# Two stacked transformer blocks on one core: the next stage's first weights are loaded and split at another place

## What is computed

```python
def first_block(...):                       # two layers
    for i in range(DEPTH):
        a = rms_norm(h, attn_norm[i])
        proj = a @ w_in[i]                  # differential attention, SSD and GLA mixers
        ...
        h = h + mix @ w_out[i]
        f = rms_norm(h, ffn_norm[i])
        h = h + (jax.nn.silu(f @ w_ffn_gate[i]) * (f @ w_ffn_up[i])) @ w_ffn_down[i]
        h = h + jax.nn.sigmoid(h @ ple_w_gate[i]) * (p[i] @ ple_w_proj[i])

def second_block(...):                      # four layers: sb, moba, swa, sb
    for i in range(DEPTH_2):
        mod = c_act @ ada_w[i] + ada_b[i]
        sh1, sc1, g1, sh2, sc2, g2 = ...    # split of mod
        h = modulate(rms_norm_2(x, norm_gain[i, 0]), sh1, sc1)
        y = one of stick_breaking / moba / swa_sink attention
        x = x + g1 * y
        h = modulate(rms_norm_2(x, norm_gain[i, 1]), sh2, sc2)
        x = x + g2 * swiglu(h, ffn_w_gate[i], ffn_w_up[i], ffn_w_down[i])
```

## Time and profile before

| | |
|---|---|
| median of three runs | 2336.67 us (2335.86 to 2341.69) |
| the profiled execution | 2342.8 us, span 2341.0 us |
| granted PE clock, mean | 0.979 |
| PE matmul busy | 2185.9 us, 93% |
| PE weight loads busy | 2075.4 us, 89% |
| DVE busy | 1598.4 us, 68% |
| ACT busy | 1092.3 us, 47% |
| chain that ended last | PE 80%, DVE 9%, ACT 5%, DMA 2%, DVE's and SP's queues 3% |
| memory read | 433.82 MB, 186 GB/s over the span |

### The profile page before, as it was taken

One profiled execution on the slowest core, in us unless ns is written; L12 is line 12 of the kernel. 1 busy time (PEld: TensorE's weight loads), 2 busy tenths in 40 slices (PEclk: granted clock), 3 DMA queues, 4 the chain that ended last, 5 costly groups with the idle time before them and its releaser, 6 DMA issues.

```text
span 2341.0 us, 44967 instructions
## 1 busy us (share of the span) xinstructions
PE 2185.9 (93%) x17588; PEld 2075.4 (89%) x17588; DVE 1598.4 (68%) x2655; ACT 1092.3 (47%) x1752; POOL 0.2 (0%) x4
## 2 busy tenths in 40 slices
PE   5889999998899999898999999999988999998998
PEld 4779899987798999898999888999887999897998
DVE  4676587756756877566778766778777854666554
ACT  3545444445454443455444455544465444555443
POOL 0000000000000000000000000000000000000000
PEclk8999999999999999999999999999999999999999
DMA  4464399934653998444599544699543965542664
GB/s 125 107 162 147 104 303 300 292 100 110 166 158 104 302 299 282 117 143 138 189 301 297 184 145 131 215 300 298 169 127 122 291 193 166 144 134 83 191 185 135
DMA packets 545379, 436.40 MB, mean 186 GB/s; under 512 B 27472, under 2 KB 470904, under 8 KB 545144
## 3 DMA queue, kind: packets, MB, share of 16 engines
q1 hardware_dynamic: 541904, 431.21, 60.5%
q10 hardware_dynamic: 3368, 3.71, 0.5%
HBM read 433.82 MB, written 1.05 MB: 186 GB/s over the span
## 4 chain that ended last, share of the span: by engine, by line
PE 80%; DVE 9%; ACT 5%; DMA 2%; DVEq 2%; issue 1%; SPq 1%; ACTq 1%
PE bank L644 12%; PE bank L646 12%; PE bank L645 12%; PE acc L644 7%; PE acc L646 7%; PE acc L645 7%; PE bank L788 3%; PE bank L1160 2%; PE bank L844 2%; ACT w_hi L1284 2%; DVE w_lo L1734 1%; PE bank L654 1%; PE bank L709 1%; PE bank L710 1%; PE bank L713 1%
## 5 line engine op out<-in xcount | busy, mean ns | idle before, releaser
L1284 ACT ACTIVATE w_hi<-wslot 128x1024 fp32r<-128x1024 f32 x590 | 610.5, 1054 | 534.2 <-PE acc L646 253.5
L644 PE MATMUL bank<-h_hi,w_hi 128*128 128x256 f32 x2784 | 792.5, 285 | 27.3 <-DVE w_lo L1734 10.6
L645 PE MATMUL bank<-h_lo,w_hi 128*128 128x256 f32 x2784 | 778.3, 280 | 0.0
L646 PE MATMUL bank<-h_hi,w_lo 128*128 128x256 f32 x2784 | 778.3, 280 | 0.0
L1734 DVE TENSOR_TENSOR w_lo<-wslot,w_hi 128x1024 fp32r<-128x1024 f32 x412 | 494.2, 1221 | 219.4 <-ACT w_hi L1284 218.8
L644 PEld LDWEIGHTS bank<-h_hi,w_hi 128*128 128x128 f32 x2784 | 525.7, 189 | 45.4 <-DVE w_lo L1728 14.1
L645 PEld LDWEIGHTS bank<-h_lo,w_hi 128*128 128x128 f32 x2784 | 529.1, 190 | 2.2 <-issue 1.7
L646 PEld LDWEIGHTS bank<-h_hi,w_lo 128*128 128x128 f32 x2784 | 526.5, 189 | 0.0
L644 PE MATMUL acc<-mid_hi,w_hi 128*128 128x256 f32 x1120 | 317.7, 284 | 7.8 <-DVE mid_lo L2279 4.6
L646 PE MATMUL acc<-mid_hi,w_lo 128*128 128x256 f32 x1120 | 312.6, 279 | 0.0
L645 PE MATMUL acc<-mid_lo,w_hi 128*128 128x256 f32 x1120 | 312.6, 279 | 0.0
(11 more groups left out here) (286 smaller groups left out, 2987.1 us busy)
## 6 DMA issues: line engine op xcount, KB each, us to landing
wslot<-in_ada_w_dram SPq DMA_DIRECT2D x192, 512.0 KB, 5.7
wslot<-in_ffn_w_gate_dram SPq DMA_DIRECT2D x88, 512.0 KB, 4.9
wslot<-in_ffn_w_up_dram SPq DMA_DIRECT2D x88, 512.0 KB, 5.4
wslot<-in_ffn_w_down_dram SPq DMA_DIRECT2D x88, 512.0 KB, 3.7
wslot<-in_w_in_dram SPq DMA_DIRECT2D x72, 512.0 KB, 4.8
wslot<-in_sb_w_in_dram SPq DMA_DIRECT2D x48, 512.0 KB, 4.5
wslot<-in_w_ffn_gate_dram SPq DMA_DIRECT2D x44, 512.0 KB, 4.7
wslot<-in_w_ffn_up_dram SPq DMA_DIRECT2D x44, 512.0 KB, 5.4
```

What stands on the lines that cost most here:

```text
L644: pe.matmul(dst, w_hi[:, w, cols], hi, start=start, stop=False, skip_group_check=True)
L645: pe.matmul(dst, w_hi[:, w, cols], lo, start=False, stop=False, skip_group_check=True)
L646: return pe.matmul(dst, w_lo[:, w, cols], hi, start=False, stop=stop, skip_group_check=True)
L1284: return act.activation(dst, src, ACT.Copy)
```

## The change

It moves steps at the seams between stages; the arithmetic stays. In words:

- **SP.** The first two attention units of the next layer are issued in the last `two_steps` of the ffn, between its halves (`next_loads`), for moba, swa and sb. In the first stack the two projection units go to the same place, and ple's gate units 0 and 1 are issued in the ple phase, ahead of unit 2. After ple the attention units stay where they were.
- **ACT.** Behind a second-stack ffn the two copies stand ahead of the table load. In ple all five first gate units are copied behind the split of x; the next attention's two units are copied behind the sigmoids of gates 5 and 6 (`first_high`), pairs 0 and 1 of the squares are taken behind those of gates 3 and 5, pairs 2 and 3 behind the last (`square_pair`), all with the sigmoid's table loaded. The norm after ple has no squares and no copies left.
- **DVE.** The two attention units are split at the end of the ffn, ahead of the adds, or behind ple's tiles 6 and 7. For moba and swa ("late") the second half of the last ada block is multiplied in the norm phase and stored behind the h loop.
- **PE.** For these two the last `ada_sum` stands behind the warming matmuls, and the first v projection waits for `ada_stored`.

```diff
@@ schedule, norm
-        phase("norm", counts, split=split, **more)
+        prior, kinds = phases[-1][0], [kind for kind, _, _ in phases]
+        early = split == "att" and prior != "setup"
+        late = None
+        if early:
+            was = phases[-1][2] if prior == "ple" else phases[len(kinds) - 1 - kinds[::-1].index("ffn")][2]
+            was.update(att_at=dict(at), att=more["att"], att_layer=more["layer"])
+            if prior != "ple" and ada_blocks(was["ada"]) == ADA_STEPS:
+                late = was["ada"], was["start"]
+        phase("norm", counts, split=split, early=early, late=late, squared=prior == "ple", **more)
...
@@ sync
+                    for n in range(2 if ph["early"] and not ph["squared"] else 0, 3):
+                        first_load(ph["att"], ph["layer"], n, at)
...
+                    def next_loads():
+                        for n in range(2):
+                            if ph["stack"] == 1:
+                                used = ph["next"].get(f"slot{SLOT_PROJ + n}", 0)
+                                load(SLOT_PROJ + n, wslot[:, SLOT_PROJ + n, :], a["ple_w_proj"][ph["layer"]][P * n:P * n + P, :], used + 1)
+                            elif ph["att"]:
+                                first_load(ph["att"], ph["att_layer"], n, ph["att_at"])
...
+                    def two_steps(cols, rows, need, layer, acol, aneed, last=False):
                         for b in range(2):
+                            if last and b:
+                                next_loads()
...
-                    if ph["stack"] == 1:
-                        ple_unit(0, ph["layer"], ph["next"])
-                        ple_unit(1, ph["layer"], ph["next"])
-                        for n in range(2):
-                            used = ph["next"].get(f"slot{SLOT_PROJ + n}", 0)
-                            load(SLOT_PROJ + n, wslot[:, SLOT_PROJ + n, :], a["ple_w_proj"][ph["layer"]][P * n:P * n + P, :], used + 1)
...
                 elif kind == "ple":
-                    for m in range(2, KT):
+                    for m in range(KT):
@@ tensor
                     keep_warm(1, 4)
+                    if ph["late"]:
+                        ada_sum(ph["late"][1], ADA_STEPS - 1)
...
-                    if blocks == ADA_STEPS:
+                    if blocks == ADA_STEPS and ph["stack"] == 1:
                         ada_sum(at, blocks - 1)
@@ scalar
-                    for q in range(4):
-                        act.wait_ge(sem["x_ready"], g("x_ready") - 3 + q)
-                        act.activation(sqT[:, 2 * q:2 * q + 2, :], xT[:, 2 * q:2 * q + 2, :], ACT.Square)\
-                           .then_inc(sem["squares"], 1)
+                    for q in range(0 if ph["squared"] else 4):
+                        square_pair(q, g("x_ready") - 3 + q)
...
-                    ple_high(2, at)
                     act.wait_ge(sem["down_done"], g("down_done"))
-                    ple_high(3, at)
-                    ple_high(4, at)
+                    for m in range(MIX_PARTS):
+                        ple_high(m, at)
...
                         if m + 5 < KT:
                             ple_high(m + 5, at)
+                        if m in (5, 6):
+                            first_high(ph["att"], m - 5, ph["att_at"])
+                        if m in (3, 5):
+                            square_pair(m // 2 - 1, g("x_ready") + m // 2)
+                    for q in (2, 3):
+                        square_pair(q, g("x_ready") + q + 1)
@@ vector
+                    if ph["late"]:
+                        ada, start = ph["late"]
+                        for n in (2, 3):
+                            ada_unit(start, ada, ADA_STEPS - 1, n, True)
...
+                    if ph["late"]:
+                        ada_store(start, ada, ADA_STEPS - 1)
...
-                    for m in range(2 if ph["stack"] == 1 else 0):
-                        low(PLE_SLOTS[m], PLE_PARTS[m], ph["next"]["w_high"] + m + 1)
+                    for n in range(2):
+                        if ph["att"] and ph["stack"] == 2:
+                            first_low(n, ph["att_at"])
...
-                    for m in (2, 3, 4):
+                    for m in range(MIX_PARTS):
                         ple_low(m)
...
+                        if m >= 6:
+                            first_low(m - 6, ph["att_at"])
```

## The result

The changed kernel takes 2310.95 us (median of 4 runs, 2306.06 to 2321.20) beside 2336.27 us for the kernel before (4 runs, 2334.89 to 2341.69): a ratio of 0.9897 with the interval 0.9863 to 0.9930. A second measurement with five runs gave 2311.82 us and 0.9867 (0.9847 to 0.9888). The forecast was 2309.3 us, 0.9883. The gain is some 25 to 29 us where 27.4 were summed up.

A forecast was written before the change was run, and what follows sets the result against it. TensorE, busy 93% of the span, was taken as the bound, so only its stalls and cold clock could give time. Gains of 12.0 + 3.8 + 3.3 + 0.3 + 8.0 = 27.4 us off the median 2336.67 gave 2309.3 us, range 2302 to 2319.

The forecast's parts named there:

- Ple to norm: Two passages from ple to attention norm: copies and squares hidden among the gates, sums start without a stall; 6.0 us each.
- rival 3: In ple: Square needs another table than Sigmoid's and reloads tables; 2314 us; chance 0.12 together with rival 2.
- Moba: Second-stack ffn to moba's norm: earlier loads, copies and splits, with ada products moved behind the adds, gain 3.8 us.
- Swa: Second-stack ffn to swa's norm: as at moba with less idle time, half-width loads slower but with room; gain 3.3 us.
- rival 1: The queue: moved loads delay down 21, losing 3.1 us at each of five seams, 16 in all; 2325 us; chance 0.11.
- Sb: Second-stack ffn to sb's norm, without ada work: gain 0.3 us, with -1.2 and +1.2 as ends.
- I take these 1.2 us as won: At sb: ACT's 1.19 us wait for down 21 would vanish with two attention loads gone ahead.
- Ends of the first-stack ffns: Two ffn ends before ple: four loads leave the front, so gate and up come sooner; 3.6 and 4.4, together 8.0 us.
- The cover of 0.5 us for the gates: In ple: splits of gate units 0 and 1 finish 0.5 us before the projection ends; failure costs up to 2.4 us a stage.
- rival 2: In ple: gates start late, splits of units 0 and 1 ending behind the projection; 2.4 us twice, 2314; chance 0.12 with rival 3.
- Rival 4: Slower than before: down 21 lands 4.5 us late, the clock falls too, five seams lose 5.5 us each; chance 0.04.
- Rival 5: The change does little: squares still end last because x does, leaving 8.0 us or less, 2329; chance 0.05.

The follow-up runs named there:

- E1: The changed kernel keeping only the passages from ple to norm (squares among the gates, attention units behind gates 5 and 6), the rest as before: 2325.92 us, ratio 0.9928.
- E4: The changed kernel, but the four squares after ple stay in the norm phase; copies and splits stay moved: 2318.93 us, ratio 0.9921.
- E5: The changed kernel, but for moba and swa the last ada block is computed in the ffn's tail again: 2317.30 us, ratio 0.9921.
- E6: The changed kernel, but the projection units and swa's second unit are issued behind down 21, ahead of the last two ada loads: 2318.11 us, ratio 0.9911.
- E9: The changed kernel, but swa's second unit is issued behind down 21 and the projection units behind the last ada loads: 2313.98 us, ratio 0.9875.
- E0: The changed kernel run again unaltered, measured against the kernel before: 2311.82 us, ratio 0.9867.
- E3: The changed kernel keeping only the second-stack seams (moba, swa, sb, last ada block late), the rest as before: 2335.06 us, ratio 0.9969.
- E8: The changed kernel, but ple's gate units 0 and 1 are also loaded between the halves, four loads ahead of down 21: 2315.16 us, ratio 0.9899.
- E2: The changed kernel keeping only the moved loads at the ends of the first-stack ffns, the rest as before: 2332.25 us, ratio 0.9960.
- E7: The changed kernel, but the two moved loads go one half earlier, ahead of gate 21, up 21 and down 20: 2305.87 us, one run.

## Why the prediction held, and which of its terms did not

**Ple to norm, 12.0 forecast, 12.5 measured.** The mechanism is shown by E1 and E4, down to the table load, hidden behind the sums and done at 499.08 us. The prediction had the sums end 3.7 us behind the end of the gates (501.1 - 497.4); they take 3.61 us, without a break.

**Square under Sigmoid's table** (rival 3): no load between sigmoids, so 0 was right and the 5 us were not lost. The Trainium skill (ScalarE: Activation LUTs, What ACT_TABLE_LOAD costs) puts a change of set at 2.66 us, of which 1.28 us are the load and the rest a drain. The load took 1.28 us here too, but it started 0.01 us behind the last square (497.80) and the next operation 0.11 us behind its end (499.19), so that the drain is not seen.

**Moba, 3.8 forecast, 3.6 measured.** Each step stands in the rows above. The prediction had the exchange on DVE (two splits where four products stood) in its sum, but gave it no price of its own. E5 gives it: without that exchange the seam is 1.6 us slower than before.

**Swa, 3.3 forecast, 1.2 to 1.3 measured: the term that was off.** The prediction said of the half-width loads: "slower, but has 7 us". SP and ACT in the changed kernel:

```profile
1631.11 0.47 SPq L464 DMA_DIRECT2D wslot<-in_swa_w_in_dram  x1
1631.62 4.79 SPq L482 DMA_DIRECT2D wslot<-in_swa_w_in_dram  x2
1638.21 0.34 SPq L464 DMA_DIRECT2D wslot<-in_ffn_w_down_dram  x1
1638.60 1.87 SPq L464 DMA_DIRECT2D wslot<-in_ada_w_dram  x2
1640.51 1.88 SPq L482 DMA_DIRECT2D wslot<-in_swa_w_in_dram  x2
```

```profile
1643.28 1.06 ACT L1306 ACTIVATE w_hi<-wslot 128x1024 fp32r<-128x1024 f32 x1 [1.38 <-DMA wslot<-in_ffn_w_down_dram]
```

SP spends 4.79 us on issuing the two half-width loads of the second unit (moba's two whole units took 1.16 us together), and it has 1.80 us left before down 21's slot comes free. It is not set by the loads' form alone: behind down 21, in E6 and E9, the same two took SP 1.06 us. Down 21, issued at 1638.21, is waited for until 1643.28, 5.07 us, and TensorE stands 0.98 us for its mid_lo. What the DMA engines do meanwhile (TensorE busy, clock, DMA share, GB/s), at swa from the issue of down 21 to its landing, and at moba before and behind it:

```profile
1638.00:1643.00 5.00, 5.00 (x45) 1.00 1.12 295
```

```profile
1286.00:1290.00 4.00, 4.00 (x36) 1.00 1.13 339
1290.00:1294.00 4.00, 4.00 (x37) 1.00 0.93 282
```

The hole of the earlier trace rows, 0.22 busy, is full at both. At moba the share has fallen to 0.93 while down 21 is on its way; at swa it is still 1.12, with 295 GB/s where moba's full stretch has 339. This is rival 1's mechanism, at the seam where the prediction said it came near, at 1.2 us and not 3.1. E6 and E9 move the second unit behind down 21 and the wait is gone. That wait is the whole of what is missing behind silu 21: from there to the first query it is 17.20 us before, and 15.44, 16.13, 15.14, 15.46 and 14.69 us in the changed kernel, E0, E3, E4 and E8. The gain and ACT's wait for down 21 together make 3.1 us in each of the five, and E6 and E9, without the wait, gain 3.0 and 3.2. So the 3.3 us held but for this wait, which the term had put at nothing.

**Sb, 0.3 forecast, 0.5 to 0.9 measured.** "I take these 1.2 us as won" rested on one landing. E1 and E2 leave sb as before and had waits of 0.21 and 0.20 us, and distances of 29.65 and 29.61: as short as in the changed kernel. TensorE's pace (the last section) is in these numbers too: from silu 19 to silu 21 the kernel before and E0 took 16.96 us, the changed kernel, E1 and E2 16.32, so that 0.64 of the 0.85 us are the pace's. And where down 21 came as late with the change as before it (1.13 us in E9, 1.19 before), silu 21 to the first product took 14.20 us against 13.43: the two splits ahead of the adds then cost, as the lower end of the forecast had it. So what the change does for sb can't be told from nothing, and the 1.19 us of the earlier trace rows were that execution's.

**Ends of the first-stack ffns, 8.0 forecast, 8.5 measured, in both profiles.** The waits of the earlier trace rows are gone. What is late next in the first stage is down 20 (ACT waits 2.88 us) and TensorE's 0.9 us for mid_lo, neither of them in E0; in the second stage TensorE waits for nothing from 883 to 925 us. The cover of 0.5 us for the gates held: from 424 to 480 us TensorE waits for that mid_lo and 0.3 us for an ada sum, and for no split of a gate (rival 2 false).

**Rival 1** came true clearly at swa alone; at the first projection the waits scatter too much to tell. Its sign, ACT waiting over 1 us for a down load, stood at two of the five seams in the first profile (swa and the first ffn's end), not in most. Its price, 7.29 us over four loads or 1.8 us each, was a little high: ACT waits 1.40 us for that gate with nothing in front, so that four cost 5.9 us, and two cost 3.1 us in E7 (4.47 against 1.40), 1.5 us each in both. What was wrong in it was to let each of five seams pay. The Trainium skill (DMA: Bandwidth & Descriptors, Issuing engines are not separate DMA queues) has the loads of all issuing engines interleave on the same 16 DMA engines. The delay at four loads (3.14 us in E8) agrees with it, but all loads here leave from SP, and no run tells interleaving from mere order in a queue; at moba two in front cost ACT 0.3 us on average. **Rival 4** fell: no wait for down 21 with two loads in front was over 2.2 us, half of the 4.5 it needed. **Rival 5** fell with E1. What the clock does behind a stall was priced as certain at 1.79 us; E4 has it once and not the other time, and in E2 and E3 the sums took up to 6.20 us, 2.6 more than at full clock.

**The sum.** 26.8 us where 27.4 were forecast is closer than the terms are. Swa's 2.0 us too many stand against 0.5 at the passages, 0.5 at the ends of the first-stack ffns and 0.5 at sb, the last of which is mostly TensorE's pace; that they nearly cancel is luck. The timed gains, 25.3 and 29.2 us, are too wide apart to tell such terms.

## What to carry to other kernels

- Price a load in front by the load behind it: what it delays, and how much slack that one has. Here the gate had three microseconds and down 21 half of one, and a hole in the queue took two plain loads but not four, nor one plain and two narrow ones.
- When work is moved ahead of something that sets the pace, find what can leave from the same stretch. The splits moved alone (E5) made the seams slower than they were; with the ada products moved out behind them moba's gained 3.6 us and swa's 1.2.
- A wait on a DMA seen in one execution is not yet a cost: look at how the same load lands in other executions before counting it as won.

## What the runs showed of the hardware that was not expected

TensorE has two paces at full granted clock, and which one a stretch gets differs from execution to execution of one program. The last ffn, from its first to its last silu, in the changed kernel and in E0 (the same program), ACT's rows:

```profile
2124.25 0.38 ACT L1693 ACTIVATE silu_g<-bank 128x256 f32<-128x256 f32 x1 [3.17 <-PE bank L731]
...
2290.81 0.38 ACT L1693 ACTIVATE silu_g<-bank 128x256 f32<-128x256 f32 x1 [4.07 <-PE bank L664]
```

```profile
2126.10 0.39 ACT L1693 ACTIVATE silu_g<-bank 128x256 f32<-128x256 f32 x1 [3.17 <-PE bank L731]
...
2299.05 0.39 ACT L1693 ACTIVATE silu_g<-bank 128x256 f32<-128x256 f32 x1 [4.29 <-PE bank L664]
```

166.56 us and 172.95 us. Fifty microseconds of it, busy time and count of matmuls, granted clock, DMA share and GB/s, first in the changed kernel, then in E0:

```profile
2150.00:2200.00 50.00, 50.00 (x444) 1.00 0.65 190
```

```profile
2150.00:2200.00 50.00, 50.00 (x427) 1.00 0.63 185
```

Both are full, both at a granted clock of 1.00, and one does 4% more: 50 / 444 = 0.1126 us a matmul against 50 / 427 = 0.1171. In the twelve profiled executions the last ffn took 166.6 us seven times and 172.9 five times, with nothing between, whatever the kernel; the eight gates of ple take 16.66 or 17.31 us in the same way. This is more than the 8.6 us between the profiled executions and the medians, though no row tells the pace of the timed runs: the last two ffns took 176.58 and 172.95 us in the profile of before, 172.86 and 166.56 in that of after, 10.1 us less, of which the change has no part, since E0 has before's numbers again. 0.6 of these 10.1 us lie behind silu 19 of the ffn before sb, within sb's distance; the other 9.5 and the 26.8 us of the seams make 36.2 us. The remaining 2.3 us, the other way, lie in stages whose code is the same, 1.1 us ahead of the first ffn and 1.5 us between the first ple and the second ffn above all; these two stages differ by 1.2 and 2.6 us between the two profiles of the changed kernel as well. It is likely also why one program's runs spread over 15 us, but no row shows that. What sets the pace stays open: neither the granted clock nor the DMA share of the rows tells the two apart. For reading a profile it means that spans are compared seam by seam, or between executions whose undisturbed stretches have the same length.
